# Three of 190 weight tiles loaded in six pieces, ten rows on eight DMA engines and six on the other eight

## The chip, the cores and the metric

The kernel runs on one core of a Trainium2 chip (trn2). The metric is the device time of one execution in microseconds (us), lower is better. The core has 16 DMA engines, which all the queues of the core share; a transfer into on-chip memory (128 partitions) is cut into packets, and here a packet of the large loads is one partition's row.

## The reference, cut to what matters

An encoder trunk of one layer on 512 tokens of width 2048, float32. After a mixing stage (Fourier, spatial gating, short convolution, pooling), each token is routed to two of 32 experts, and each expert is a gated MLP of hidden width 768:

```
w_gate: (1, 32, 2048, 768)   w_up: (1, 32, 2048, 768)   w_down: (1, 32, 768, 2048)
a = jax.nn.silu(xblk @ w_gate[e]) * (xblk @ w_up[e])
return a @ w_down[e]
```

The three weight tensors of the experts are 604 MB, and each byte is read from HBM once. That is nearly all that the kernel moves.

## The kernel before

Up to about 545 us the mixing stage runs, with its own smaller weights. Then comes the expert stage: 32 experts, two of them a pair. The weights of one expert are six tiles (`PARTS = 6`: gate in two halves, up in two, down in two), 192 tiles in all. A tile is 128 partitions by 6144 floats, so a row of a tile is 24,576 bytes, contiguous in HBM and in its partition, and a tile is 3072 KB.

SyncE issues the tiles in one queue, in order. They go into a ring of five slots (`RING = 5`, a sixth is used once at the start). Before it issues tile n, SyncE waits on `tile_used` until TensorE has used up the tile that held the slot. So about four tiles are always queued or in flight. `tile(n)` calls `weight(...)`, which issues one DMA for the whole tile that adds 16 to the slot's semaphore `tile_landed[s]` when all of it has landed. The last two tiles are loaded in five pieces of their own.

TensorE takes the tiles in the same order: `landed(n)` waits until the slot's semaphore has its count, then `gate_up` or `down` runs its matmuls on the tile. VectorE, ScalarE and GpSimd do short work between (activation, row gathers of 128 tokens per pair, sums) and are mostly idle. GpSimd's gathers are DMAs too, once per pair.

Tile n belongs to expert n // 6 and is part n % 6 of it. Tiles 36, 96 and 156, which the change touches, are the first half of the gate weights of experts 6, 16 and 26, and all three go into slot 0, which is part of the memory that the trace calls `region_rest`.

Of the kernel before, what the change touches and what calls it, by code (L numbers as in the profile page):

```python
# [30 lines left out]
P = 128  # L31
# [35 lines left out]
QK = KT // 2  # L67
DK = FT // 2
PARTS = 6
# [11 lines left out]

def added(c, t):
    return ADDS.index((c, t)) + 1


def nth_tile(n):
    return divmod(n, PARTS) if n < TILES - 2 * PARTS else TAIL[n - (TILES - 2 * PARTS)]
# [8 lines left out]
def build(nc, x, mix_norm, w_in, w_fourier, w_spatial, b_spatial, conv_w, w_pool, pool_scale, out_norm,  # L96
# [3 lines left out]
    with ctx:  # L100
        def sem(name):
            return ctx.enter_context(nc.semaphore(name))
# [98 lines left out]
        ring_gu = [r.rearrange("p (a b) -> p a b", a=QK) for r in ring]  # L201
# [45 lines left out]
        def slot_of(n):  # L247
            return n if n <= RING else (n - RING - 1) % RING
# [12 lines left out]
        wg_v = w_gate[0].rearrange("e (p k) n -> e p k n", k=KT)  # L261
# [14 lines left out]
        final_landed = sem("final_landed")  # L276
        tile_landed = [sem(f"tile_landed{s}") for s in range(RING + 1)]
        last_landed = [sem(f"last_landed{k}") for k in range(len(LAST))]
        last_down, last_hi, last_lo = sem("last_down"), sem("last_hi"), sem("last_lo")
        last_sum, last_added, f_redone, f_pre = sem("last_sum"), sem("last_added"), sem("f_redone"), sem("f_pre")  # L280
        over_landed = [sem(f"over_landed{s}") for s in range(PARTS)]
# [49 lines left out]
        def _(sp):  # L331
# [56 lines left out]
            def weight(expert, part, slot, landed):  # L388
                if part < 4:
                    src = (wg_v, wu_v)[part // 2]  # L390
                    q = part % 2
                    sp.dma_start(ring_gu[slot], src[expert, :, q * QK:(q + 1) * QK, :]).then_inc(landed, 16)
                else:
                    sp.dma_start(ring_down[slot], wdn_v[expert, part - 4]).then_inc(landed, 16)

            def tile(n):
                s = slot_of(n)
                weight(*nth_tile(n), s, tile_landed[s])

            def save_columns(n):  # L400
# [6 lines left out]
            for u in (37, 38):  # L407
                raw_unit(u)
            sp.wait_ge(y_normed, KT)
            tile(0)  # L410
            for u in (39, 40):
                raw_unit(u)
# [3 lines left out]
            save_columns(2)  # L416
            sp.wait_ge(w_ready, UNITS)
            tile(1)

            def save_last(t):  # L420
# [3 lines left out]
            for t in range(NT - 1):  # L424
                save_last(t)
            sp.wait_ge(w_used, UNITS)
            tile(2)
            save_last(NT - 1)
            tile(3)
# [45 lines left out]
        def _(pool):  # L475
# [94 lines left out]
            for t in range(NT):  # L570
                pool.wait_ge(last_added, added(0, t))
                g.tensor_tensor(gained[:, t, :], x_sb[:, t, 0:FINAL], final_row[:, 0:FINAL], ALU.mult).then_inc(f_gained, 1)
# [3 lines left out]
        def _(ae):  # L576
# [173 lines left out]
            for t in (0, 1):  # L750
                ae.wait_ge(last_added, added(0, t))
                square_first(t, f_pre, 2 * t + 1)
# [13 lines left out]
            def rms_last(t):  # L766
                ae.wait_ge(last_added, max(added(0, t), added(1, t)))
                if t < NT - 1:
                    src, junk_t, pre = x_sb[:, t, HALF:], junk3[3 + t], stat[:, 16 + t:17 + t]
                else:  # L770
                    src, junk_t, pre = x_sb[:, t, :], junk4, eps
                a.activation(junk_t, src, ACT.Square, accum_out=stat[:, t:t + 1]).then_inc(f_sq, 1)
                ae.wait_ge(f_sq, t + 1)
                a.activation(stat[:, NT + t:NT + t + 1], stat[:, t:t + 1], ACT.Sqrt, bias=pre, scale=1.0 / D).then_inc(f_rms, 1)
# [19 lines left out]
        def _(pe):  # L794
# [361 lines left out]
            def down_early():  # L1156
                for q in (0, 1):
                    slot = landed(TILES - 4 + q)
                    for kk in range(DK):
                        for c in (0, 1):  # L1160
                            for n in (0, 1):
                                j = 2 * c + n
                                mm = t_.matmul(ps[n * SLOTS:(n + 1) * SLOTS, 6 + c, :], aT[:, kk, q * SLOTS:(q + 1) * SLOTS],
                                               ring_down[slot][:, kk, j * 512:(j + 1) * 512],
                                               start=(q == 0 and kk == 0), stop=(q == 1 and kk == DK - 1))
                    mm.then_inc(tile_used, 1)
# [59 lines left out]
            def landed(n):  # L1226
                s = slot_of(n)
                pe.wait_ge(tile_landed[s], 16 if n <= RING else 16 * ((n - 1) // RING + 1))
                return s

            plan(0, True)
# [2 lines left out]
            for e in range(E):  # L1234
                i, b = divmod(e, 2)
                n = e * PARTS if e < E - 1 else TILES - 8
                if e == E - 1:
                    pe.wait_ge(at_ready, e)
                for part in range(4):
                    if part < 2:  # L1240
                        pe.wait_ge(hte_ready, 2 * e + part + 1)
                    gate_up(part, landed(n + part))
                    if i and part in ((0, 1) if b else (1, 2)):
                        pe.wait_ge(hte_ready, 2 * e + 2)
                        combine(i - 1, 2 * b + (part if b else part - 1))
                if i:
                    pe.wait_ge(comb_added, 8 * (i - 1) + 4 * b + 4)
                if not b:
                    if i + 1 < PAIRS:
                        plan(i + 1)  # L1250
                    transpose_rows(i, 1)
                elif i + 1 < PAIRS:
                    transpose_rows(i + 1, 0)
                transpose_act(e)
                if e < E - 2:
                    pe.wait_ge(at_ready, e + 1)
                    if e:
                        pe.wait_ge(m_lo_ready, 2 * e)
                    for part in (4, 5):
                        down(b, part, landed(n + part))  # L1260
# [575 lines left out]
```

## Time and profile before

| | |
|---|---|
| median of 3 runs | 2021.54 us (2020.7 to 2023.21) |
| the profiled execution's own time | 2022.05 us |
| its span in the profile | 2020.3 us |
| mean granted TensorE clock, share of full speed | 0.972 |
| TensorE busy with matmuls | 1848.6 us, 92% of the span |
| bytes moved by DMA | 681.12 MB |
| rate in the expert stage | 428 to 431 GB/s in nearly every fortieth of the span |

The span is 1.75 us shorter than the profiled execution's time, and that execution is 0.5 us above the median. A matmul's end is modelled in the profile, so a high busy share of TensorE alone doesn't say that TensorE sets the time. The digits of the DMA row give the busy share of the 16 engines in tenths, 9 is 90% or more.

### The profile page before, as it was taken

The page shows a single profiled execution, that of the slowest core. Times are in us where ns is not written, and L with a number is a line of the kernel's source. Part 1 is how long each engine was busy: PE and PEld are TensorE (multiplying, and loading weights), DVE is VectorE, ACT ScalarE, POOL GpSimd, SP SyncE. Part 2 cuts the span into 40 slices and gives each one's busy share as a digit, 9 for nine tenths or more (in the row PEclk, how much of TensorE's full clock was granted, in tenths as well). Part 3 has the DMA queues.
Part 4 walks back from the last instruction along what each step waited for, and adds up shares of the span by engine and source line. Part 5 has one row for each costly group of instructions (what it writes and reads, how often), then busy time and mean ns, then how long its engine had stood idle before and what let it go on. Part 6 is the DMA issues. An engine that isn't in the chain of part 4 may idle for free.

```text
span 2020.3 us, 20896 instructions
## 1 busy us (share of the span) xinstructions
PE 1848.6 (92%) x9414; PEld 1053.7 (52%) x9414; DVE 594.9 (29%) x839; ACT 182.7 (9%) x274; POOL 249.7 (12%) x100
## 2 busy tenths in 40 slices
PE   8999999999969999898988989989889989898896
PEld 7887878788844444344333434434344444433342
DVE  3221656621142223222222223222212312222224
ACT  4000110101110000000000010000001000000003
POOL 4333535434200000000000000000000000000001
PEclk9999999999979999999999999999999999999998
DMA  7222133443389999999999999999999999999995
GB/s 275 83 79 84 63 104 89 164 173 122 112 330 430 428 431 429 428 430 428 430 431 429 430 428 431 428 430 428 431 429 429 429 430 430 429 429 430 429 428 215
DMA packets 68746, 681.12 MB, mean 337 GB/s; under 512 B 10352, under 2 KB 13616, under 8 KB 42416
## 3 DMA queue, kind: packets, MB, share of 16 engines
q1 hardware_dynamic: 65792, 671.16, 79.7%
q0 software_dynamic: 2304, 8.39, 1.0%
q8 instruction: 76, 1.25, 0.3%
q10 hardware_dynamic: 560, 0.21, 0.0%
q14 instruction: 14, 0.11, 0.0%
HBM read 679.73 MB, written 8.39 MB: 341 GB/s over the span
## 4 chain that ended last, share of the span: by engine, by line
PE 54%; DMA 44%; DVE 1%; ACT 1%; issue 0%; SPq 0%; DVEq 0%; ACTq 0%
DMA region_rest<-in_w_gate 25%; PE banks L1203 20%; PE banks L814 15%; PE banks L1008 9%; DMA region_w<-in_w_gate 8%; DMA region_h<-in_w_gate 6%; PE banks L1141 3%; DMA region_rest<-in_w_up 3%; PE banks L1221 2%; DMA region_rest<-in_w_down 1%; PE banks L892 1%; PE banks L904 1%; PE banks L841 1%; DMA region_h<-x_rows,region_rest 1%; PE banks L1126 0%; PE banks L1039 0%
## 5 line engine op out<-in xcount | busy, mean ns | idle before, releaser
L1203 PE MATMUL banks<-region_rest,region_w 128*64 128x384 f32 x2464 | 423.9, 498 | 60.5 <-DMA region_rest<-in_w_gate 47.1
L1203 PEld LDWEIGHTS banks<-region_rest,region_w 128*64 128x64 f32 x2464 | 185.5, 139 | 290.5 <-issue 222.5
L1659 DVE TENSOR_TENSOR region_x<-banks,region_x 128x1024 f32<-128x1024 f32 x120 | 141.3, 1219 | 596.1 <-PE banks L1141 596.1
L814 PE MATMUL banks<-split_h,split_w 128*128 128x512 f32 x864 | 273.6, 394 | 0.5 <-DVE split_w L1311 0.5
L494 POOL TENSOR_TENSOR split_w<-region_rest,split_w 128x2048 fp32r<-128x2048 f32 x42 | 196.9, 4688 | 302.8 <-DVE split_w L1318 302.8
L1221 PE MATMUL banks<-region_rest,region_w 128*64 128x512 f32 x864 | 205.3, 630 | 17.9 <-DVE region_w L1685 12.3
L814 PEld LDWEIGHTS banks<-split_h,split_w 128*128 128x128 f32 x864 | 162.2, 188 | 35.1 <-issue 1.0
L549 POOL DMA_INDIRECT region_h<-x_rows,region_rest x16 | 16.0, 1002 | 1270.8 <-PE banks L1126 1259.7
L814 PE MATMUL banks<-split_w 128*128 128x512 f32 x432 | 168.2, 389 | 0.0
L1203 PE MATMUL banks<-region_w 128*64 128x384 f32 x832 | 144.8, 502 | 20.2 <-DMA region_w<-in_w_gate 17.7
L1008 PE MATMUL banks<-split_w,split_h 128*128 128x512 f32 x512 | 159.2, 392 | 0.0
L1203 PE MATMUL banks<-region_h,region_w 128*64 128x384 f32 x800 | 134.3, 488 | 15.6 <-DMA region_h<-in_w_gate 11.9
L1221 PEld LDWEIGHTS banks<-region_rest,region_w 128*64 128x64 f32 x864 | 62.4, 144 | 147.9 <-issue 116.6
L1665 DVE TENSOR_TENSOR split_w<-banks,split_w 64x1024 fp32r<-64x1024 f32 x60 | 73.2, 1220 | 184.6 <-ACT split_w L709 183.7
L1141 PE MATMUL banks<-split_w 128*128 128x512 f32 x480 | 126.7, 406 | 0.0
L1318 DVE CAST split_w<-region_rest 128x2048 fp32r<-128x2048 f32 x43 | 53.1, 1235 | 209.7 <-PE banks L814 118.5
L1203 PEld LDWEIGHTS banks<-region_w 128*64 128x64 f32 x832 | 62.9, 140 | 98.8 <-issue 79.9
L1141 PEld LDWEIGHTS banks<-split_w 128*128 128x128 f32 x480 | 85.4, 188 | 51.6 <-issue 35.9
L1008 PEld LDWEIGHTS banks<-split_w,split_h 128*128 128x128 f32 x512 | 95.4, 188 | 22.5 <-issue 3.1
L1203 PEld LDWEIGHTS banks<-region_h,region_w 128*64 128x64 f32 x800 | 58.6, 137 | 88.6 <-issue 68.1
L715 ACT ACTIVATE region_w<-banks,region_rest 128x384 f32<-128x384 f32 x32 | 18.6, 582 | 909.8 <-PE banks L1203 909.8
L1008 PE MATMUL banks<-split_w 128*128 128x512 f32 x256 | 99.7, 389 | 0.0
(236 smaller groups left out, 1257.2 us busy)
## 6 DMA issues: line engine op xcount, KB each, us to landing
region_rest<-in_w_gate SPq DMA_DIRECT2D x39, 3072.0 KB, 31.3
region_rest<-in_w_up SPq DMA_DIRECT2D x38, 3072.0 KB, 30.9
region_rest<-in_w_down SPq DMA_DIRECT2D x36, 3072.0 KB, 31.1
region_h<-in_w_up SPq DMA_DIRECT2D x13, 3072.0 KB, 29.9
region_w<-in_w_up SPq DMA_DIRECT2D x13, 3072.0 KB, 30.2
region_w<-in_w_down SPq DMA_DIRECT2D x13, 3072.0 KB, 31.1
region_w<-in_w_gate SPq DMA_DIRECT2D x13, 3072.0 KB, 30.9
region_h<-in_w_down SPq DMA_DIRECT2D x13, 3072.0 KB, 31.3
```

Of the source, the lines that this page charges most:

```text
L494: g.tensor_tensor(w_lo[u % 2], raw[u % RAW], w_hi[u % 2].bitcast(F32), ALU.subtract).then_inc(w_ready, 1)
L814: mm = t_.matmul(ps[:, 4 * (c % 2) + m, :], w[s][:, kk, cols_m], h[:, k, :], start=(k == 0 and w is w_hi and h is h_hi), stop=(k == KT - 1 ...
L841: mm = t_.matmul(ps[:, m, :], w[0][:, kk, m * P:(m + 1) * P], h[:, kk, :], start=(kk == 0 and w is w_hi and h is h_hi), stop=False)
L892: mm = t_.matmul(half, ab[:, s, h, c * HD:(c + 1) * HD], dft[:, c, s, :], start=(c == 0 and a == 0), stop=(c == 1 and a == 1))
L904: mm = t_.matmul(ps[:, m, :], wf[:, k, m * P:(m + 1) * P], fT[:, k, :], start=(k == 0), stop=(k == NH - 1))
L1008: mm = t_.matmul(ps[:, 4 * ((n + 1) % 2) + t, :], y[:, k, rows_t], w[s][:, kk, :], start=(k == 0 and y is y_hi and w is w_hi), stop=(k == ...
L1141: mm = t_.matmul(ps[:, 2 + 2 * c + n, :], back[c][:, t * P:(t + 1) * P], y[c][:, n * 512:(n + 1) * 512], start=(y is m_hi), stop=(y is m_lo))
L1203: mm = t_.matmul(ps[h * SLOTS:(h + 1) * SLOTS, u, 0:HF], hTe[:, k, :], ring_gu[slot][:, kk, h * HF:(h + 1) * HF], start=(k == 0), stop=(k ...
L1221: mm = t_.matmul(ps[g * SLOTS:(g + 1) * SLOTS, 6 + n, :], aT[:, kk, q * SLOTS:(q + 1) * SLOTS], ring_down[slot][:, kk, (2 * c + n) * 512:( ...
L1318: v.tensor_copy(w_hi[u % 2], raw[u % RAW]).then_inc(w_hi_ready, 1)
L1659: v.tensor_tensor(tile, ps[:, 2 + 2 * c:4 + 2 * c, :], tile, ALU.add).then_inc(comb_added, 1)
L1665: v.tensor_tensor(y_rows(m_lo, b, c), ps[g * SLOTS:(g + 1) * SLOTS, 6:8, :], y_rows(m_hi, b, c).bitcast(F32), ALU.subtract).then_inc(m_lo_ ...
```

## The change

Tiles 36, 96 and 156 are no longer loaded by one DMA of 128 rows but by six: the upper 64 partitions; the 32 odd partitions of the lower half; and four of 8 partitions each, 8 apart (0, 8, ..., 56, then 2, 10, ..., 58, then from 4, then from 6). The same bytes land in the same places. The first of the six adds to the slot's old semaphore, the other five to a new one, `rest_landed`, which TensorE waits for as well before it uses one of these three tiles. The change's own words say how the rows fall on the DMA engines: ten rows on each of 8 engines and six on the rest, where a whole tile puts eight on each.

```diff
+EVEN = (36, 96, 156)
...
+        rest_landed = sem("rest_landed")
...
             def tile(n):
                 s = slot_of(n)
+                if n in EVEN:
+                    src = wg_v[n // PARTS, :, 0:QK, :]
+                    sp.dma_start(ring_gu[s][64:P], src[64:P]).then_inc(tile_landed[s], 16)
+                    sp.dma_start(ring_gu[s][1:64:2], src[1:64:2]).then_inc(rest_landed, 16)
+                    for r in range(0, 8, 2):
+                        sp.dma_start(ring_gu[s][r:64:8], src[r:64:8]).then_inc(rest_landed, 16)
+                    return
                 weight(*nth_tile(n), s, tile_landed[s])
...
             def landed(n):
                 s = slot_of(n)
                 pe.wait_ge(tile_landed[s], 16 if n <= RING else 16 * ((n - 1) // RING + 1))
+                if n in EVEN:
+                    pe.wait_ge(rest_landed, 80 * (EVEN.index(n) + 1))
                 return s
```

On SyncE, around tile 36, the order before was this: the two down tiles of expert 5, then the two gate tiles of expert 6 (tiles 36 and 37), then its first up tile. Each row waits for its slot to be free.

```order
L394 DMA region_w<-in_w_down 128x6144 [waits tile_used]
L394 DMA region_rest<-in_w_down 128x6144 [waits tile_used]
L392 DMA region_rest<-in_w_gate 128x6144 [waits tile_used] x2
L392 DMA region_h<-in_w_up 128x6144 [waits tile_used]
L392 DMA region_w<-in_w_up 128x6144 [waits tile_used]
```

Now, at the same place, with the changed kernel's line numbers:

```order
L398 DMA region_w<-in_w_down 128x6144 [waits tile_used]
L398 DMA region_rest<-in_w_down 128x6144 [waits tile_used]
L404 DMA region_rest<-in_w_gate 64x6144 [waits tile_used]
L405 DMA region_rest<-in_w_gate 32x6144
L407 DMA region_rest<-in_w_gate 8x6144 x4
L396 DMA region_rest<-in_w_gate 128x6144 [waits tile_used]
L396 DMA region_h<-in_w_up 128x6144 [waits tile_used]
```

Tile 36 is now six issues in a row. Only the first waits, and no other transfer stands between them.

On TensorE, where tile 36 is used first, the order before was this:

```order
L1221 MATMUL banks<-region_rest,region_w 64x512 [waits tile_landed4]
L1221 MATMUL banks<-region_rest,region_w 64x512 x11
L1203 MATMUL banks<-region_rest,region_w 64x384 [waits tile_landed0,hte_ready]
L1203 MATMUL banks<-region_rest,region_w 64x384 x15
L1203 MATMUL banks<-region_rest,region_w 64x384 [waits tile_landed1,hte_ready]
```

And in the changed kernel it is this:

```order
L1232 MATMUL banks<-region_rest,region_w 64x512 [waits tile_landed4]
L1232 MATMUL banks<-region_rest,region_w 64x512 x11
L1214 MATMUL banks<-region_rest,region_w 64x384 [waits rest_landed,tile_landed0,hte_ready]
L1214 MATMUL banks<-region_rest,region_w 64x384 x15
L1214 MATMUL banks<-region_rest,region_w 64x384 [waits tile_landed1,hte_ready]
```

Nothing has moved on TensorE; the first of the sixteen matmuls on the tile waits for one semaphore more.

## Rows read from the trace of the kernel before

**Rows 1.** The page: rate and busy share of the DMA engines, forty slices.

```profile
PEclk9999999999979999999999999999999999999998
DMA  7222133443389999999999999999999999999995
GB/s 275 83 79 84 63 104 89 164 173 122 112 330 430 428 431 429 428 430 428 430 431 429 430 428 431 428 430 428 431 429 429 429 430 430 429 429 430 429 428 215
```

**Rows 2.** DMA queues, 600 to 1980 us: packets, MB, share of 16 engines.

```profile
DMA packets 29777, 592.14 MB, mean 429 GB/s; under 512 B 4173, under 2 KB 4173, under 8 KB 5072
...
q1 hardware_dynamic: 27557, 583.16, 98.7%
q0 software_dynamic: 2160, 8.04, 1.4%
q8 instruction: 54, 0.88, 0.3%
q14 instruction: 6, 0.05, 0.0%
```

**Rows 3.** SyncE's waits, 600 to 1980 us: us in total, times, longest.

```profile
SPq L392 <- PE banks L1203: 622.1, 93, 8.1
SPq L392 <- PE banks L1221: 275.9, 30, 12.1
```

**Rows 4.** TensorE's waits, the same stretch: us in total, times, longest.

```profile
PE banks L1203 <- DMA region_rest<-in_w_gate: 47.1, 24, 3.6
PE banks L1221 <- DVE region_w L1685: 19.5, 30, 0.7
PE banks L1203 <- DMA region_w<-in_w_gate: 17.7, 9, 2.4
PE banks L1203 <- DMA region_rest<-in_w_up: 13.2, 9, 2.0
PE banks L1203 <- DMA region_h<-in_w_gate: 11.9, 7, 3.0
```

**Rows 5.** The chain that ended last, 795 to 850 us: start, us, what.

```profile
805.59 5.41 PE banks L1203 x32
810.99 0.02 issue
811.01 31.34 DMA region_rest<-in_w_gate
842.35 0.14 issue
842.48 5.39 PE banks L1203 x32
```

**Rows 6.** SyncE's issues around tiles 36, 96 and 156: start, us.

```profile
802.60 8.73 SPq L392 DMA_DIRECT2D region_rest<-in_w_gate  x2
818.32 0.33 SPq L392 DMA_DIRECT2D region_h<-in_w_up  x1
...
1253.52 7.67 SPq L392 DMA_DIRECT2D region_rest<-in_w_gate  x2
...
1700.38 0.33 SPq L392 DMA_DIRECT2D region_rest<-in_w_gate  x1
```

**Rows 7.** Line 392, SyncE's issues: ns min/median/max, first and last start; us to landing.

```profile
L392 SPq DMA_DIRECT2D region_rest<-in_w_gate x39: 327/328/504, 445.9 to 1917.4; - x39
...
DMA to landing us min/median/max: 10.1/31.0/33.7
```

## The prediction, made before the changed kernel ran

> **What bounds the kernel now.** I read the page's slices first. From the thirteenth on, that is from about 600 us, the DMA row is at 9 and the rate stands at 428 to 431 GB/s to the last slice but one [rows 1]. TensorE's clock is at full there but for single slices, so it isn't the clock that sets the pace. The question is whether the 16 DMA engines are the bound in the stage in which the three tiles lie. The queues of that stage say yes: SyncE's queue, which carries the weight tiles, holds 98.7% of the time of 16 engines, the gathers 1.4% and instruction loading 0.3% [rows 2]. That adds up to a little over 100, since packets of different queues overlap on one engine. There is no free DMA time.
>
> Then who waits for whom. SyncE waits long for TensorE before it issues (622 and 276 us) [rows 3], but this is the ring at work: a tile takes a median of 31.0 us from issue to landing [rows 7], four times the 7.35 us that one takes at the full rate (below), so a queue of some three tiles always stands before the engines and SyncE's waits cost nothing. TensorE in turn waits for landings, 47.1 + 17.7 + 13.2 + 11.9 us and smaller ones in this stage [rows 4]. In the chain of waits, a DMA of 31.34 us, then 5.39 us of matmuls on that tile, then the next DMA [rows 5]: each round is five tiles of DMA. TensorE needs less time for a tile than the DMA engines do, so what is added to the slowest DMA engine is added to the end, and what is taken from it comes off.
>
> **The price of a row.** In 600 to 1980 us SyncE's queue moved 583.16 MB [rows 2], which is 23,729 rows of 24,576 bytes, in 98.7% of 16 engines times 1380 us = 21,793 us: 0.918 us a row. Eight rows, a tile's share of one engine, take 7.35 us.
>
> **The change, part by part, for one changed tile.**
>
> The issue. SyncE issues six DMAs instead of one, five more at 0.33 us [rows 7], 1.6 us. The next tile's issue stood 7 to 8 us behind tile 36 and the one after that 15.7 us behind [rows 6], each held by its slot, and behind all of them lies a queue of over 20 us. Cost nothing; were that queue gone, 1.6 us a tile, 5 us in all. Semaphore writes of 4 bytes, 16 for each whole DMA, are among the 4173 packets under 512 B [rows 2]; with five more DMAs they are a fraction of a row. The second wait on TensorE ends in time if the tile lands in time, and costs nothing by itself. If it comes late, the 16 matmuls on the tile are queued behind it, then every later tile, and SyncE for the slot.
>
> The count of rows. Eight engines get two rows more, eight get two less: per tile +1.84 us on the former, -1.84 us on the latter, over three tiles +5.5 and -5.5 us. This is worth something only if the engines aren't equally late now. Something in the stage isn't spread by rows: 54 instruction packets at 0.3% of 16 engines' 1380 us [rows 2], 66 us, 1.23 us each. No row says on which engines they run. On all 16, none is behind. On eight only, each costs its engine at least 1.23 us, and at most half a row more, 0.46, since on a full engine a row is always under way that it has to share with: 1.23 to 1.69. I take 1.6, near the upper end, because the engines are full and the shares of the queues do overlap [rows 2]. Then the eight are 54 x 1.6 / 8 = 10.8 us behind the others at the end of the stage (bounds 8.3 and 11.4). If the ten rows go to those that are ahead, the late ones end 5.5 us earlier, and the others at 5.5 - 10.8 = -5.3 against the last engine's end now: a gain of 5.3 us from the count of rows alone.
>
> Where the rows land. A whole tile fills all 128 partitions, and 16 engines move 430 GB/s with it [rows 1], 26.9 each, with no room left [rows 2]. No large transfer of this trace fills fewer than 128, so what a half costs isn't shown. Its bounds: below, nothing, if an engine's pace depends on its own rows alone. Above, double time, if the partitions have doors as the engines have lanes: eight engines' worth of doors for each half, and two engines that write through one door take turns. By the upper bound: the upper 64 rows (4 on each engine) cost 4 rows more on every engine, the odd lower ones (2 on each) 2 more. The four DMAs of 8 rows put eight engines on eight partitions of the lower half at once, and by the upper bound these meet two by two as well: 4 rows more for the eight engines that take them. Sum on a ten-row engine, 2 + 4 + 2 + 4 = 12 rows, 11.0 us a tile, 33.0 us for three. On a six-row engine -2 + 4 + 2 = 4 rows, 3.7 us a tile, 11.0 us for three.
>
> I take a value near the upper bound. The row nearest to it is the rate itself: engines and partitions are filled to 430 GB/s by a pattern in which each engine has eight partitions to itself, and nothing in it shows the partitions to have twice the room of the engines that feed them. It is a choice, not a reading.
>
> The Trainium skill, "SBUF — State Buffer", section "Door 1: The DMA port swizzle", speaks against this change: it says that a partition range that stays in one half reaches 8 of 16 ports, and gives 196 GB/s for 64 partitions against 328 for 128 at 1 MiB. By those figures a half tile takes 1.67 times its time rather than 2. No row here shows it. Its table has partitions 0 to 3 and 32 to 35 on one port, by which rows 0 and 32, 8 and 40, and so on, meet.
>
> Ten-row engines end 33.0 us later, less the lead. If they are those without instruction packets, they have 10.8 us in hand: 33.0 - 10.8 = 22.2 us later than the last engine ends now, and the six-row ones 11.0 later. The later sets the end: 22 us. Since the engines can drift apart by some us within the queue, not every pair meets in a half, and the 22 are rather the upper side of this case.
>
> The skill's "DMA: Bandwidth & Descriptors", section "Why a DMA increments its semaphore by 16 and not by 1", says that on SyncE's queue a DMA whose outer size allows only k engines runs on the lowest-numbered k. The split into ten and six agrees with eight for 8 rows; which engines load instructions it doesn't say, and no row does.
>
> The sum against its own time: 2022.05 us in the profiled execution, 0.5 above the median. From the median, 2021.5 + 22 = 2043.5 us, 1.1% slower.
>
> **The rivals.**
>
> *Rows alone count, and the ten-row engines are those that are ahead.* For it: the instruction packets are a load of the right size that the rows don't carry. Against: it needs the lower bound of the unknown price, and no row shows the grouping. It gives -5.3 us, 2016.2. This is the one on the other side. Its place is the three tiles, its price the two rows moved, and the point from which it decides follows from the same counts: if a row in a shared half costs a share s more (0 alone, 1 for double time), a ten-row engine ends at 5.5 + 27.5 s - 10.8 (ten such rows a tile, 30 x 0.918 = 27.5) and a six-row one at -5.5 + 16.5 s. The kernel gets faster as long as s is under 0.19.
>
> *Rows alone count, but the ten fall on the engines that load instructions,* or these packets are on all 16 and no engine is ahead. +5.5 us, 2027.0. Nothing in the rows chooses between this side and the other.
>
> *The two cancel.* A small price of the shared half, s from about 0.05 to 0.34, puts the ten-row engines within 4 us of the present end. It gives 2021.5. For it: doors with some room beyond what the engines feed. Against: it is a narrow part of what is possible.
>
> *Sharing in full on the wrong side.* The ten-row engines are the late ones: +33.0 us with no lead to take off, 2054.5; with some pairs missing each other, 30 us, 2051.5.
>
> **How the numbers follow.** Sharing at or near double time, ten rows on the engines that are ahead: 0.50, 2043.5. Sharing in full on the late ones: 0.10, 2051.5. Rows alone, ten on those ahead: 0.28, 2016.2. Rows alone, other side: 0.05, 2027.0. Cancelled: 0.07, 2021.5. About 0.2% (4 us) is what a measurement of this kernel can tell from no change. With a little of each neighbour falling inside it: faster 0.29, same 0.09, slower 0.62. The likeliest case's own range is 2032 (the six-row engines' 11.0 alone) to 2047 (a lead of 8.3, 33.0 - 8.3 = 24.7). For 8 in 10 over all cases the range has to hold the gain on the low side and the edge of the full case on the high side: 2015.5 to 2050.
>
> **What would show it.** In the profile of the changed kernel: if sharing is right, the rate in the slices at tiles 36, 96 and 156 (issued near 803, 1254 and 1700 us before [rows 6]) drops under 425 GB/s, with the DMA row still at 9, since packets in shared partitions last longer; the share of the 16 engines' time of SyncE's queue at the same bytes rises; the tile's own DMAs take 40 us and more to landing instead of 31; TensorE has waits of 7 to 11 us for them where the longest is 3.6 now [rows 4]. If rows alone count, the rate stays at 430, no long wait appears, and the span shrinks by about 5 us, spread over the stage as shorter waits of TensorE. The prediction is wrong if those three slices look as before. It is wrong in size if the waits come but the lead or the meetings are other than taken: then the first tile's wait (11.0 us of turns, least lead) and the last one's tell by how much.

## The result, and the profile after

The changed kernel takes 2078.0 us, the kernel before 2021.7 us: a ratio of 1.0278 (95% interval 1.0264 to 1.0292), 56 us slower. The prediction had the side right. Its size was 22 us and the upper end of its range 2050 us; the measured loss is two and a half times that size and lies outside the range. In the two profiled executions the spans differ by 51.1 us.

The page of the changed kernel, its forty slices and its queues (packets, MB, share of 16 engines):

```profile
span 2071.4 us, 20911 instructions
...
DMA  7222222543399999999999999999999999999994
GB/s 268 82 81 78 81 87 88 192 169 122 137 381 430 430 429 404 353 430 430 429 429 429 429 429 379 372 431 428 430 429 430 429 430 336 358 429 429 430 425 171
...
q1 hardware_dynamic: 65936, 671.16, 80.0%
```

The rate stands at 430 as in [rows 1] but for three dents, and these are at the three tiles. The DMA row stays at 9 in them: the engines are busy and move less. SyncE's queue moved the same 671.16 MB, but it held 80.0% of 16 x 2071.4 us, where before it held 79.7% of 16 x 2020.3 us. That is 26,514 against 25,763 engine-us, 751 more, or 47 us on each of 16 engines. Nearly all of the 51 us is packets that take longer, not idle time.

The first dent close up, in stretches of 10 us, for the changed kernel and then for the kernel before. Each line has the stretch and its length, the busy time of TensorE's matmuls, TensorE's weight loads, VectorE, ScalarE and GpSimd (with the number of instructions), then TensorE's granted clock, the busy share of the DMA engines and GB/s.

```profile
815.00:825.00 10.00, 9.35 (x57) 4.71 (x55) 2.37 (x4) 0.00 (x0) 0.00 (x0) 1.00 1.06 390
825.00:835.00 10.00, 2.61 (x12) 0.79 (x10) 0.00 (x0) 0.00 (x0) 0.00 (x0) 0.73 0.97 170
835.00:845.00 10.00, 7.19 (x23) 1.77 (x20) 1.68 (x2) 2.04 (x2) 0.00 (x0) 0.76 0.98 219
845.00:855.00 10.00, 7.84 (x38) 3.54 (x40) 0.77 (x1) 0.00 (x0) 0.00 (x0) 0.83 0.99 413
```

```profile
825.00:835.00 10.00, 7.12 (x34) 1.93 (x29) 0.75 (x1) 1.78 (x2) 0.00 (x0) 1.00 1.00 430
835.00:845.00 10.00, 7.90 (x48) 4.08 (x50) 1.70 (x2) 0.26 (x1) 0.00 (x0) 1.00 1.00 428
```

For 10 us all engines together move 170 GB/s, 40% of the rate before, at a share of 0.97. Half the doors would give 215. So this isn't only the halving that the prediction priced, and it lasts 20 us, not the 7 of one tile.

The packets in the two traces say it row by row. Of the rows of 24,576 bytes that start between 825 and 835 us, the kernel before has 175, and each takes 0.91 to 0.93 us. The changed kernel has 69 there, and each takes 1.73 to 2.72 us. None goes at the old pace, and not all of them belong to tile 36: the last engine's share of tile 35, a whole tile, landed at 833.8 us in place of 827.7, while the first engine's share of it landed at 823.3 us, as before (823.5).

How much is lost at each place can be read from SyncE's issues a few tiles behind it (start, us), here of the seventh tile behind each of the three, first in the changed kernel, then before:

```profile
866.82 0.33 SPq L396 DMA_DIRECT2D region_h<-in_w_gate  x1
...
1330.16 0.33 SPq L396 DMA_DIRECT2D region_h<-in_w_gate  x1
...
1803.98 0.33 SPq L396 DMA_DIRECT2D region_h<-in_w_gate  x1
```

```profile
855.26 0.33 SPq L392 DMA_DIRECT2D region_h<-in_w_gate  x1
...
1302.94 0.33 SPq L392 DMA_DIRECT2D region_h<-in_w_gate  x1
...
1751.53 0.33 SPq L392 DMA_DIRECT2D region_h<-in_w_gate  x1
```

The differences are 11.6, 27.2 and 52.5 us: the places cost 11.6, 15.7 and 25.2 us. The same edit gets dearer each time, and the first place is the one that fits the prediction's 11.0 us. The prediction had said that the first place against the last would tell by how much its size is off.

TensorE's waits for landings are where this reaches the end (us in total, times, longest; 600 to 2040 us):

```profile
PE banks L1214 <- DMA region_rest<-in_w_gate: 58.2, 22, 11.3
PE banks L1232 <- DMA region_rest<-in_w_down: 25.3, 6, 9.1
```

The longest wait is 11.3 us where it was 3.6 [rows 4]. In the chain of waits of the changed kernel, the round that holds tile 36 is a DMA of 43.16 us (start, us, what):

```profile
810.75 43.16 DMA region_rest<-in_w_gate
853.91 0.14 issue
854.05 5.39 PE banks L1214 x32
```

The same round took 31.34 us before [rows 5], 11.8 less. It is tile 37, a whole tile that is queued behind the pieces.

### The profile page after: what moved, and what is told of

It is laid out like the page before. It is cut to its first block, busy times and chain, and to the rows that moved or that the text cites. A ratio compares the mean times of both kernels' runs of the same rounds, so it can differ in the third digit from the quotient of the medians.

```text
span 2071.4 us, 20911 instructions
## 1 busy us (share of the span) xinstructions
PE 1872.9 (90%) x9414; PEld 1060.3 (51%) x9414; DVE 594.4 (29%) x839; ACT 182.6 (9%) x274; POOL 249.6 (12%) x100
## 3 DMA queue, kind: packets, MB, share of 16 engines
q1 hardware_dynamic: 65936, 671.16, 80.0%
q8 instruction: 76, 1.25, 0.2%
## 4 chain that ended last, share of the span: by engine, by line
PE 54%; DMA 43%; DVE 1%; another core or an unknown queue 1%; ACT 1%; issue 0%; SPq 0%; DVEq 0%; ACTq 0%
DMA region_rest<-in_w_gate 24%; PE banks L1214 20%; PE banks L825 14%; PE banks L1019 8%; DMA region_w<-in_w_gate 8%; DMA region_h<-in_w_gate 6%; DMA region_rest<-in_w_down 3%; PE banks L1152 3%; PE banks L1232 3%; DMA region_rest<-in_w_up 2%; PE banks L903 1%; PE banks L915 1%; PE banks L852 1%; PE banks L1137 1%; DMA region_h<-x_rows,region_rest 1%
## 5 line engine op out<-in xcount | busy, mean ns | idle before, releaser
L1214 PE MATMUL banks<-region_rest,region_w 128*64 128x384 f32 x2464 | 431.4, 505 | 73.2 <-DMA region_rest<-in_w_gate 58.2
L1214 PEld LDWEIGHTS banks<-region_rest,region_w 128*64 128x64 f32 x2464 | 187.3, 142 | 308.7 <-issue 247.1
L1232 PE MATMUL banks<-region_rest,region_w 128*64 128x512 f32 x864 | 222.0, 673 | 37.1 <-DMA region_rest<-in_w_down 25.3
L1232 PEld LDWEIGHTS banks<-region_rest,region_w 128*64 128x64 f32 x864 | 66.8, 154 | 179.7 <-issue 131.6
L1214 PE MATMUL banks<-region_h,region_w 128*64 128x384 f32 x800 | 134.3, 488 | 10.6 <-DMA region_h<-in_w_gate 6.3
## 6 DMA issues: line engine op xcount, KB each, us to landing
region_rest<-in_w_up SPq DMA_DIRECT2D x38, 3072.0 KB, 30.2
```

The source lines that it names most:

```text
L1214: mm = t_.matmul(ps[h * SLOTS:(h + 1) * SLOTS, u, 0:HF], hTe[:, k, :], ring_gu[slot][:, kk, h * HF:(h + 1) * HF], start=(k == 0), stop=(k ...
L1232: mm = t_.matmul(ps[g * SLOTS:(g + 1) * SLOTS, 6 + n, :], aT[:, kk, q * SLOTS:(q + 1) * SLOTS], ring_down[slot][:, kk, (2 * c + n) * 512:( ...
```

## The experiments

All times are medians; ratios are against the kernel before, measured on the same chip beside each. All kernels load every byte, except one that says otherwise.

**Two halves and nothing else.** Eight rows on every engine again.

```diff
                     sp.dma_start(ring_gu[s][64:P], src[64:P]).then_inc(tile_landed[s], 16)
-                    sp.dma_start(ring_gu[s][1:64:2], src[1:64:2]).then_inc(rest_landed, 16)
-                    for r in range(0, 8, 2):
-                        sp.dma_start(ring_gu[s][r:64:8], src[r:64:8]).then_inc(rest_landed, 16)
+                    sp.dma_start(ring_gu[s][0:64], src[0:64]).then_inc(rest_landed, 16)
...
-                    pe.wait_ge(rest_landed, 80 * (EVEN.index(n) + 1))
+                    pe.wait_ge(rest_landed, 16 * (EVEN.index(n) + 1))
```

> Tiles 36, 96 and 156 in two DMAs, upper 64 and lower 64 partitions: eight rows on each engine again, all bytes loaded. Theory A (two engines that write to one half take turns in pairs, nothing else): 8 rows of 0.918 us at double time on each engine, +7.3 us a tile, +22 us in all. Theory B (a half held up by its doors holds up every engine, those that write elsewhere too, for as long as any transfer of a half is under way): as much as the whole change, +13 to +19 us a tile, +40 to +56 us. Theory C (the number of DMAs, six a tile, costs the time): one DMA more a tile, under +3 us.

2067.3 us against 2021.3, ratio 1.0224 (1.0209 to 1.0240): +46 us. One DMA more a tile and no uneven split make most of the loss. Its dent close up:

```profile
825.00:835.00 10.00, 2.93 (x10) 0.77 (x8) 0.00 (x0) 0.00 (x0) 0.00 (x0) 0.66 1.00 182
835.00:845.00 10.00, 5.89 (x20) 1.51 (x16) 2.44 (x2) 2.04 (x2) 0.00 (x0) 0.82 1.02 194
```

Theory A, double time for the halves' own rows, is out as the whole account: it gives 22 us. Theory C is out.

**The number of DMAs, first try.** Six DMAs, each over all 128 partitions.

```diff
+                    sp.dma_start(ring_gu[s][:, :, 0:128], src[:, :, 0:128]).then_inc(tile_landed[s], 16)
+                    for c in range(128, DE, 128):
+                        sp.dma_start(ring_gu[s][:, :, c:c + 128], src[:, :, c:c + 128]).then_inc(rest_landed, 16)
```

> Tiles 36, 96 and 156 in six DMAs of all 128 partitions, each a sixth of the row (4096 bytes in place of 24,576): the change's number of DMAs and semaphores and its wait, without any transfer of a part of the partitions. Theories A and B: within 4 us of before. Theory C (number of DMAs): near the full change, +50 us.

2030.7 us against 2021.3, ratio 1.0047 (1.0032 to 1.0063): +9.4 us. That excludes 50 us, but it isn't clean. The pieces ran across the row, so each row went in 48 packets of 512 bytes, not in six of 4096 as the expectation says, and 1.0047 mixes both. In this trace a packet of 512 bytes takes 27 ns, so 48 take 1.3 us where one row of 24,576 bytes takes 0.91.

**The number of DMAs, again.** Eight pieces, each a contiguous eighth of the row.

```diff
+                    sp.dma_start(ring_gu[s][:, 0:1], src[:, 0:1]).then_inc(tile_landed[s], 16)
+                    for k in range(1, QK):
+                        sp.dma_start(ring_gu[s][:, k:k + 1], src[:, k:k + 1]).then_inc(rest_landed, 16)
```

> The number of DMAs again, without the small packets of the first try (there the pieces ran across the row, so its packets were 512 bytes and not the 4096 that its expectation says; it cost 9.4 us): tiles 36, 96 and 156 in eight DMAs of all 128 partitions, each one contiguous eighth of the row, 3072 bytes, with the second semaphore. Sharing alone explains the settled split's 30.2 us, so the number of DMAs should cost nothing: within 3 us of before. If a DMA costs the queue 0.33 us or more: +7 us or more.

2023.8 us against 2022.2, ratio 1.0008 (0.9999 to 1.0017). More issues, more semaphore writes and the second wait cost 1.7 us by the medians, with an interval from nothing to 3.4 us.

**Each transfer alone.** SyncE waits for an empty queue before each transfer (shown for tile 96; tiles 36, 66 and 126 are done in the same way with other pieces). `quiet()` waits until all pieces issued so far have landed. The kernel ran once, for its trace.

```diff
+                    for m in range(n - 4, n):
+                        sp.wait_ge(tile_landed[slot_of(m)], 16 * ((m - 1) // RING + 1))
...
+                    if n == 96:
...
+                        sp.dma_start(dst[64:P], src[64:P]).then_inc(rest_landed, 16)
+                        quiet()
...
+                        sp.dma_start(dst[1:64:2], src[1:64:2]).then_inc(rest_landed, 16)
+                        quiet()
+                        for r in range(0, 8, 2):
...
+                            sp.dma_start(dst[r:64:8], src[r:64:8]).then_inc(rest_landed, 16)
+                        quiet()
```

> Single transfers in an empty queue: SyncE waits until all earlier tiles have landed, then loads tile 36 whole; tile 66 as upper 64, then, that landed, lower 64 partitions; tile 96 as upper 64, then the 32 odd ones, then the four DMAs of 8 rows 8 apart together; tile 126 as upper 64 and 32 odd together, then four DMAs of 8 rows 4 apart together. All bytes are loaded; the total time is of no interest (the emptied queue costs some 20 us at each place). Read from issue to landing. Theory A or B with double time where 16 engines share 8 doors: whole tile 7.35 us plus a latency L of about 2; upper 64 also 7.3 + L in place of 3.7 + L; 32 odd 3.7 + L in place of 1.8 + L; four of 8 rows 8 apart 7.3 + L if they meet two by two, 3.7 + L if not; 4 apart 3.7 + L. If a half is no slower than its rows: 3.7, 1.8, 3.7, 3.7, each + L.

SyncE's issues in this kernel (start, us). Each waits for the landing of the one above it, so the difference of two starts is a transfer with its latency; only lines 442 and 444 are issued together. Line 420 is the whole tile 36, 424 and 427 the halves of tile 66, 431, 434 and 438 the pieces of tile 96, 442 and 444 the upper 64 and the 32 odd ones of tile 126, 448 its four DMAs 4 apart:

```profile
826.74 0.33 SPq L420 DMA_DIRECT2D region_rest<-in_w_gate  x1
836.76 0.33 SPq L396 DMA_DIRECT2D region_rest<-in_w_gate  x1
...
1056.43 0.58 SPq L424 DMA_DIRECT2D region_rest<-in_w_gate  x1
1066.58 0.49 SPq L427 DMA_DIRECT2D region_rest<-in_w_gate  x1
1076.93 0.34 SPq L396 DMA_DIRECT2D region_rest<-in_w_gate  x1
...
1296.04 0.47 SPq L431 DMA_DIRECT2D region_rest<-in_w_gate  x1
1306.16 0.47 SPq L434 DMA_DIRECT2D region_rest<-in_w_gate  x1
1312.23 2.53 SPq L438 DMA_DIRECT2D region_rest<-in_w_gate  x4
1321.85 0.34 SPq L396 DMA_DIRECT2D region_rest<-in_w_gate  x1
...
1541.07 0.51 SPq L442 DMA_DIRECT2D region_rest<-in_w_gate  x1
1541.62 0.59 SPq L444 DMA_DIRECT2D region_rest<-in_w_gate  x1
1555.72 2.71 SPq L448 DMA_DIRECT2D region_rest<-in_w_gate  x4
1562.67 0.34 SPq L396 DMA_DIRECT2D region_rest<-in_w_gate  x1
```

| | us | less the latency 2.67 | rows an engine at 0.918 | one row's packet, median us |
|---|---|---|---|---|
| whole tile, 128 rows | 10.02 | 7.35 | 7.34 | 0.91 |
| upper 64 | 10.12 to 10.15 | 7.5 | 3.67 | 1.92 |
| lower 64 | 10.35 | 7.7 | 3.67 | 1.91 |
| 32 odd of the lower half | 6.07 | 3.4 | 1.84 | 1.86 |
| four of 8 rows, 8 apart | 9.62 | 6.95 | 3.67 | 1.78 |
| four of 8 rows, 4 apart | 6.95 | 4.3 | 3.67 | 0.91 |

The latency is the whole tile's 10.02 less its eight rows of 0.918. Half a tile takes as long as a whole one. The odd rows double too, and so nearly do the 8-row DMAs 8 apart; 4 apart they don't. (The last four are issued over 2.5 to 2.7 us, which is part of what they show.) These are the prediction's doublings, and they come out as it priced them: 7.5 + 3.4 + 6.95 - 7.35 = 10.5 us more on a ten-row engine, 7.5 + 3.4 - 7.35 = 3.5 on a six-row one, where it said 11.0 and 3.7. For tile 126 the upper 64 and the 32 odd ones of the lower half, issued together, took 14.65 us, 12.0 less the latency. That is no less than one behind the other (7.5 + 3.4 = 10.9), although they write to different halves.

**Only the last tile.** `EVEN = (156,)`.

> Only tile 156 in six pieces as in the change; tiles 36 and 96 whole as before. With the change, the landings fell behind by about 12 us at tile 36, 16 more at tile 96 and 23 more at tile 156. Theory B1 (a place costs more the further the DMA engines have drifted apart, and they drift with time by themselves through the instruction packets): tile 156 alone costs 16 to 20 us. Theory B2 (the growth comes from the drift that the change itself makes, two rows more on eight engines at each earlier place): near the first place's 12 us. Theory B3 (same price everywhere): 17 us.

2041.1 us against 2022.1, ratio 1.0098 (1.0082 to 1.0113): +18.9 us. A late place is dear by itself, more than the first place's 11.6 us, without two changed tiles ahead of it. Between this and the 25.2 us that the third place costs in the full change lie 6 us. The earlier two places widen the spread of the engines ahead of tile 156 from 10.3 to 16.4 us, as shown below.

**In step.** The change with a wait before each of the three tiles, until all that is ahead has landed, and its control, the kernel before with the same three waits.

```diff
                 if n in EVEN:
                     src = wg_v[n // PARTS, :, 0:QK, :]
+                    for m in range(n - 4, n):
+                        sp.wait_ge(tile_landed[slot_of(m)], 16 * ((m - 1) // RING + 1))
```

> Control for the settled split: the kernel before, but SyncE waits before tiles 36, 96 and 156 until the four tiles ahead have landed, so that all DMA engines start these tiles in step. Each place pays for the empty queue (a latency of about 2.7 us, and what TensorE then waits, since three tiles fewer are queued): +10 to +60 us. Its time is only the base for the other.

> The changed kernel with the same three waits, so that all engines start the six pieces in step. Alone and in an empty queue the upper 64 partitions took 10.15 us, the 32 odd ones 6.07, the four of 8 rows 9.62 and the whole tile 10.02, latency of about 2.7 us included: 10.5 us more for a ten-row engine than a whole tile. Theory B1 (the rest of the 17 us a place is the drift of the engines, by which a half also meets whole tiles of other engines): 10 to 11 us a place over the control, +30 to +33 us. Theory B4 (the excess comes from the full queue, in step or not): +45 to +55 us over the control.

The control takes 2032.6 us, the split 2062.8 us: 30.2 us, 10.1 a place, against 56 us without the waits. The runs of both stood beside one another on one chip. Even with what the waits themselves cost (10.6 us), the change with them is 15 us faster than the change without. Theory B1 holds: started in step, a place costs the end what its transfers cost alone on a ten-row engine; the other 26 us come from engines that are not at the same tile. The queue behind the pieces isn't empty: SyncE issues the next three tiles within 5 us of the first piece.

The traces of the two show the two groups of engines. Tile 37, a whole one, lands on the 16 engines 16.5 to 17.3 us after tile 36's issue in the control. In the split it lands on eight engines after 24.2 to 25.0 us and on the other eight after 27.8 to 28.4 us, and the same at tiles 96 and 156. So the ten-row engines are 11.3 to 11.6 us later, as predicted (11.0), but the six-row ones 7.6 to 8.0, where the prediction said 3.7: they go on to a whole tile while the others are still at their 8-row pieces, and lose time there.

**Who is ahead.** The kernel before with three more DMAs of 8 rows from HBM to HBM behind each of the three tiles, nine rows more on each engine that such a DMA uses. No partition is written.

```diff
                 weight(*nth_tile(n), s, tile_landed[s])
+                if n in EVEN:
+                    if n > EVEN[0]:
+                        sp.wait_ge(rest_landed, 48 * EVEN.index(n))
+                    for k in range(3):
+                        sp.dma_start(spare[k], wu_v[n // PARTS, 0:8, k * 4:k * 4 + 8, :].rearrange("p k n -> p (k n)")).then_inc(rest_landed, 16)
```

> The kernel before, with extra work: behind each of the tiles 36, 96 and 156 three DMAs of 8 rows of 24,576 bytes from HBM to HBM, so three rows more on each of the eight engines that an 8-row DMA uses, nine in all, and nothing on the other eight; no partition is touched. A row priced as before is 0.918 us, 8.3 us in all. If these eight are the ones that are ahead by about 10.8 us: within 3 us of before. If they are the ones with the instruction packets, or no engine is ahead: +8 us.

> The control of the one with 8 rows: the same three extra DMAs at the same places with 16 rows each, so nine rows of HBM to HBM more on every one of the 16 engines. +8.3 us whichever engines are ahead, at 0.918 us a row; more if a row from HBM to HBM takes longer.

> As the one with 8 rows from HBM to HBM, but with 6 rows, so nine rows more on each of six engines only. The 8-row one cost 7.9 us where the free lead of those engines should have hidden it, so at least one of the eight is not ahead. If the ones not ahead are among the last two of the eight: within 3 us of before. If they are among the first six: +8 us again.

> As the extra work of 8 and 6 rows from HBM to HBM, with 4 rows a DMA: nine rows more on each of four engines. 8 rows cost 7.9 us, 6 rows 6.2. If no late engine is among the first four: within 3 us of before; if one is: +6 to +8 us.

| rows a DMA | time | before | ratio |
|---|---|---|---|
| 16 | 2029.95 | 2021.3 | 1.0041 (1.0027 to 1.0054) |
| 8 | 2029.2 | 2021.3 | 1.0035 (1.0021 to 1.0048) |
| 6 | 2028.3 | 2022.1 | 1.0030 (1.0018 to 1.0042) |
| 4 | 2021.1 | 2021.9 | 0.9994 (0.9985 to 1.0003) |

On 16 engines nine rows cost 8.65 us, near their 8.3. On the engines of a 4-row DMA they are free, so those engines are ahead by about as much as was put on them, or more. On the engines of a 6-row DMA and of an 8-row one they cost 6.2 and 7.9 us. So at least one of the late engines is among the eight that the change gives ten rows. The spreads below say how many.

**The count of rows, nearly without sharing.** Six rows' worth on every engine by whole-width DMAs, the lower half's last quarter by 8-row DMAs 4 apart. The last quarter of the upper 64 partitions of these three tiles is not loaded, so this kernel leaves out work.

```diff
+                    sp.dma_start(ring_gu[s][:, 0:6, :], src[:, 0:6, :]).then_inc(tile_landed[s], 16)
+                    for r in (0, 1, 2, 3, 32, 33, 34, 35):
+                        sp.dma_start(ring_gu[s][r:r + 29:4, 6:8, :], src[r:r + 29:4, 6:8, :]).then_inc(rest_landed, 16)
```

> The count of rows alone, with as little sharing as can be: tiles 36, 96 and 156 as one DMA of all 128 partitions and three quarters of the row (six rows' worth on each engine), then the last quarter of the lower 64 partitions as eight DMAs of 8 partitions, 4 apart, so two rows' worth on each of the eight engines of such DMAs. The last quarter of the upper 64 partitions isn't loaded; old data stands there. So the upper half's engines have two rows less a tile, the others eight as before. Theory D1 (all late engines are in the upper half): -5.5 us. Theory D2 (as the 8-row extra work says, at least one late engine is among the lower eight): within 3 us of before.

2021.2 us against 2021.9, ratio 0.9996 (0.9987 to 1.0005). Taking two rows a tile off the upper half's engines, even without giving them to anyone, gains nothing that can be measured. It is D2, and it agrees with the extra work.

**How far apart the engines are.** The kept traces answer this without a further run. Behind each engine's share of a tile stands a packet of 4 bytes, which adds one to the tile's semaphore, and the traces keep the time of each of the 16 additions. The first and the last of a tile give the spread of the engines. It is read here four tiles ahead of a changed one, before that one disturbs it, and set beside the rows that took over 1.25 us at the place (0.91 is the normal time, and a changed tile has 128 rows) and beside the cost of the place, read as above:

| place | spread, us | rows over 1.25 us | cost, us |
|---|---|---|---|
| change, started in step, each of three | about 1 | 169 to 174 | 10.1 |
| two halves, tile 36 | 3.3 | 196 | 12.7 |
| change, tile 36 | 3.8 | 178 | 11.6 |
| two halves, tile 96 | 6.7 | 247 | 15.7 |
| change, tile 96 | 9.2 | 231 | 15.7 |
| two halves, tile 156 | 9.4 | 298 | 16.6 |
| only tile 156 | 10.3 | 295 | 18.9 |
| change, tile 156 | 16.4 | 317 | 25.2 |

(In step the spread is that of the changed tile's first piece, 0.8 to 1.3 us, and the cost is a third of the 30.2 us; for only tile 156 it is the whole 18.9 us.) Within each kernel the cost rises with the spread, and so does the number of rows of other, whole tiles that are slowed. The two rows of the table with spreads near 3.5 us show that the spread isn't all: there the two halves cost 1.1 us more than the change at a smaller spread. In the kernel before the spread is 4.0, 7.0 and 10.4 us ahead of the three tiles, so most of it is there without the change, and the first two changed tiles add the 6 us that tile 156 finds on top.

What makes the spread can be read too. In the kernel before, the 16 engines' times for one tile add up to 116.9 us where nothing else runs beside it, and to 118.4 us where one packet of the instruction queue (16,384 bytes, about 1.07 us) falls in it: such a packet costs its engine 1.54 us. At tile 189, the last one that is loaded whole, seven engines are 11.2 to 12.6 us ahead of the last one, one is 8.1 ahead, and eight are within 3.0 us of it. In the kernel with 8 rows of extra work, two engines come last, 0.5 us apart, and the other fourteen are 7.2 us and more ahead of them; with 6 rows one comes last, and the others are at least 6.7 us ahead of it. So of the eight engines that get ten rows, six are ahead in the kernel before and two are late. In the kernel that loads six rows' worth on the upper half's engines, the two that come last, 1.3 us apart, are at least 4.3 us behind all others, which is why it gained nothing.

## Why the prediction was wrong

**Right: what bounds the kernel.** The DMA engines set the pace, and what was added to the slowest came out at the end. Nine rows more on all 16 engines cost 8.65 us for 8.3 us of rows, and the three dents reach TensorE as waits.

**Right: the issue, the semaphore writes and the second wait cost next to nothing.** Eight whole-width pieces a tile gave 1.0008 (0.9999 to 1.0017), 1.7 us by the medians.

**Right: the value taken for rows in a shared half.** It was called a choice, and double time is what each transfer shows alone: 10.15 us for 64 partitions, 10.02 for 128. The sums for one tile, 11.0 and 3.7 us, measured 10.5 and 3.5 with each transfer alone. In step, with more tiles queued behind, the ten-row engines' 11.0 holds and the six-row engines' 3.7 becomes 7.6 to 8.0. The Trainium skill's "SBUF — State Buffer", section "Door 1: The DMA port swizzle", says that 64 partitions of one half reach 8 of 16 ports; the times alone agree, and they are nearer to a full halving than its 196 against 328 GB/s at 1 MiB. By its table 8 rows 8 apart reach four ports and 8 rows 4 apart in one block of 32 reach eight; 9.62 against 6.95 us agrees.

**Wrong, the step that failed: the turns were priced on the three tiles' own rows.** The prediction says: "Since the engines can drift apart by some us within the queue, not every pair meets in a half, and the 22 are rather the upper side of this case." It took drift as a relief. It is the opposite. While some engines are in a half, the others are at whole tiles, and their rows are slowed too: all 16 engines together moved 170 GB/s for 10 us, less than the 215 that half the doors give, and all 69 rows that started in these 10 us took 1.73 to 2.72 us. The further apart the engines are, the longer some of them are in a half, and the more whole rows meet it: beside the 128 rows of the changed tile itself, at least 50, 103 and 189 others took over 1.25 us at the three places. The places cost 11.6, 15.7 and 25.2 us in order of time; tile 156 alone 18.9; and three places started in step 30.2 us together. So of the 56 us, about 30 are the sharing as priced, and about 26 go away when the engines start in step. The drift itself stands in the traces: ahead of the three places the engines are 3.8, 9.2 and 16.4 us apart in the changed kernel, and 4.0, 7.0 and 10.4 in the kernel before.

Why rows of whole tiles slow down too was not tested. The Trainium skill's "DMA: Bandwidth & Descriptors", section "Back-pressure in remote DMA", says of another kind of transfer that a saturated SBUF port clogs the path back to the source engines and to those that share it. The 170 GB/s would fit that, but no run here separates it from other causes.

**Wrong: the lead, 10.8 us to take off.** It was to be on all eight ten-row engines. The size was right: an instruction packet costs its engine 1.54 us, where the prediction took 1.6 of its bounds 1.23 to 1.69, and half of the engines do run 8.1 to 12.6 us ahead at the end. (Its lower bound came from a share rounded to 0.3%; the packets last about 1.07 us.) The grouping was wrong. The extra work of 8 and 6 rows cost 7.9 and 6.2 us and that of 4 rows nothing, and the landings show two late engines among the ten-row eight. With even one late engine among them there is no lead to take off: 33.0, not 22.2, by the prediction's own count. The measured 30.2 us in step is that number. The case that the prediction called "Sharing in full on the wrong side", 33.0 us with no lead, is thus the nearest of its cases, though the sides are mixed and not wrong altogether.

**The rivals.** "Rows alone count" falls twice: the price of a shared half is full, and without any sharing the level is worth 0.9996. It wouldn't have given 5.3 us. Its premise holds in part: the load which isn't spread by rows is the instruction packets, and four engines do have room for nine rows more. But the ten-row engines are not the ones that have it, so it wouldn't have come about even with rows at their own price. Two small slips changed nothing: tile 37's issue stood 8.4 us behind tile 36, not 7 to 8, and 2021.5 + 24.7 is 2046, not 2047.

**The range.** Its upper end, 2050, was drawn inside the bounds of one tile's own rows, times three. It held no case in which a slow transfer slows its neighbours in the queue, and 2078 lies there.

None of the runs shows a version faster than the kernel before: a half is dear by itself, and leveling by 8-row DMAs gives rows to two late engines. Whether rows given to the engines of a 4-row DMA, which have room for nine, would gain anything was not tried.

## What to carry to other kernels

When the DMA engines are the bound, load all 128 partitions with each transfer; a transfer of 64 costs as much as one of 128. In a full queue it can cost about as much again, because the engines are not at the same transfer, and rows of whole tiles slow too while some engines are in the narrow one. The further apart the engines are, the dearer it is. Price a transfer alone in an empty queue first, then ask who else is in the queue at that time. Before work is shifted between engines to even them out, find out which are late by giving a few of them extra work: nine free rows on four engines and none on six said more than any average over 16. And read when each engine's share of a transfer lands, if the trace keeps it: the 16 times of one tile show the spread that no average shows.

## What the runs showed of the hardware

- A load into 64 partitions of one half takes the time of one into 128: 10.15 against 10.02 us, at 24,576 bytes a row. 32 rows of one half took 6.07 us. A single row took 1.92 us there in place of 0.91.
- Four DMAs of 8 rows each took 9.62 us with the rows 8 partitions apart and 6.95 us with them 4 apart, the same bytes.
- In a full queue the 16 engines together fell to 170 GB/s from 430 while such transfers were in it, lower than half, and single rows took up to 2.72 us at the first place and 2.98 us at the third. Rows of whole tiles are among the slowed ones.
- The 16 DMA engines of one queue don't stay together: the first and the last were 4.0 us apart on tile 32 and 12.6 us on tile 189, with eight equal rows on each engine for every tile. A 16 KB instruction packet cost its engine 1.54 us.
- Rows of 24,576 bytes cut into packets of 512 bytes cost 9.4 us for three tiles of 3072 KB; cut into packets of 3072 bytes 1.7 us, with an interval that includes none.
- SyncE took 0.33 us to issue a DMA of 128 rows (0.43 when issued right behind another) and 0.47 to 0.68 us for one of 64, 32 or 8 rows, which was hidden by the queue.
